# Four one-use landing places and groups of four in the expert stage of a two-layer decoder

## The reference

```python
def swiglu(x, w1, w3, w2):
    return (jax.nn.silu(x @ w1) * (x @ w3)) @ w2

logits = (t @ w_router).astype(jnp.float32)
top_v, top_i = lax.top_k(logits, TOP_K)          # 2 of 8
top_w = jax.nn.softmax(top_v, axis=-1)
combine = jnp.sum(jax.nn.one_hot(top_i, N_EXPERTS) * top_w[..., None], axis=1)
for e in range(N_EXPERTS):
    out = out + combine[:, e:e + 1] * swiglu(t, w1[e], w3[e], w2[e])
```

## Time and profile before

| | |
|---|---|
| median of 3 runs | 1219.22 us |
| profiled execution | 1219.02 us, span 1217.2 us |
| TensorE (PE) busy | 1202.1 us, 99% |
| VectorE (DVE) / ScalarE (ACT) busy | 737.4 us / 593.7 us |
| expert stage | from 550.65 us (first product) to about 1206.5 us |
| HBM read | 379.8 MB |

### The profile page before, as it was taken

How to read it: one execution, slowest core, us unless ns; L and a number is a source line. 1 busy time by engine, 2 the same in 40 slices (tenths; PEclk the granted TensorE clock), 3 DMA queues, 4 the chain that set the end, 5 groups by cost and what they waited for, 6 DMA issues and landing times.

```text
span 1217.2 us, 15724 instructions
## 1 busy us (share of the span) xinstructions
PE 1202.1 (99%) x6377; PEld 907.8 (75%) x6377; DVE 737.4 (61%) x769; ACT 593.7 (49%) x645; POOL 67.8 (6%) x55
## 2 busy tenths in 40 slices
PE   9999999999999999999999999999999999999996
PEld 8778888888888888888777666777567776667762
DVE  6867766656445857767665745755546664566532
ACT  6667435444436467446545434544535444454430
POOL 0600001000000600000000000000000000000001
PEclk9999999999999999999999999999999999999999
DMA  9753558555554454367999999999999999999997
GB/s 378 302 197 117 182 184 295 184 202 178 184 197 173 169 177 141 136 248 275 408 425 428 385 424 416 428 428 418 424 416 430 427 421 415 427 429 426 429 423 299
DMA packets 36590, 384.82 MB, mean 316 GB/s; under 512 B 4337, under 2 KB 4337, under 8 KB 7985
## 3 DMA queue, kind: packets, MB, share of 16 engines
q1 hardware_dynamic: 34672, 374.83, 76.8%
q0 software_dynamic: 1696, 8.66, 1.9%
q10 hardware_dynamic: 144, 0.26, 0.1%
HBM read 379.80 MB, written 7.61 MB: 318 GB/s over the span
## 4 chain that ended last, share of the span: by engine, by line
PE 91%; DMA 2%; DVE 2%; issue 2%; ACT 1%; POOL 1%; SPq 0%; DVEq 0%; ACTq 0%; POOLq 0%
PE ps L621 22%; PE ps L623 21%; PE ps L622 21%; PE ps L1728 18%; PE ps L1254 3%; DMA ring<-in_pairs 1%; PE ps L1624 1%; DMA h<-in_x 1%; PE ps L1612 1%; DVE wl L616 1%; POOL rst L759 1%; PE ps L1313 1%; ACT wh L598 0%; PE ps L1600 0%; DVE mix L2088 0%
## 5 line engine op out<-in xcount | busy, mean ns | idle before, releaser
L616 DVE TENSOR_TENSOR wl<-raw,wh 128x2048 fp32r<-128x2048 f32 x170 | 391.9, 2307 | 259.8 <-ACT wh L598 259.2
L598 ACT ACTIVATE wh<-raw 128x2048 fp32r<-128x2048 f32 x170 | 325.4, 1917 | 262.5 <-PE ps L623 243.6
L621 PE MATMUL ps<-wh,XT 128*128 128x512 f32 x856 | 341.7, 399 | 1.2 <-DVE wl L616 1.1
L623 PE MATMUL ps<-wh,XT 128*128 128x512 f32 x856 | 333.8, 390 | 0.0
L622 PE MATMUL ps<-wl,XT 128*128 128x512 f32 x856 | 333.6, 390 | 0.0
L621 PEld LDWEIGHTS ps<-wh,XT 128*128 128x128 f32 x856 | 160.7, 188 | 52.2 <-issue 16.2
L623 PEld LDWEIGHTS ps<-wh,XT 128*128 128x128 f32 x856 | 160.7, 188 | 34.5
L622 PEld LDWEIGHTS ps<-wl,XT 128*128 128x128 f32 x856 | 160.9, 188 | 30.9
L616 DVE TENSOR_TENSOR wl<-ring,wh 128x2048 fp32r<-128x2048 f32 x48 | 109.9, 2290 | 79.5 <-ACT wh L598 79.2
L598 ACT ACTIVATE wh<-ring 128x2048 fp32r<-128x2048 f32 x48 | 91.9, 1914 | 101.7 <-PE ps L623 90.8
L1728 PE MATMUL ps<-raw,few_X 128*64 128x256 f32 x768 | 88.2, 382 | 0.0
(11 more groups left out here) (296 smaller groups left out, 1151.9 us busy)
## 6 DMA issues: line engine op xcount, KB each, us to landing
raw<-in_pairs SPq DMA_DIRECT2D x76, 2048.0 KB, 13.1
ring<-in_pairs SPq DMA_DIRECT2D x52, 2048.0 KB, 13.5
raw<-in_units SPq DMA_DIRECT2D x86, 1024.0 KB, 4.9
raw<-in_lasts SPq DMA_DIRECT2D x6, 1024.0 KB, 13.6
y_rows<-in_zeros POOLq DMA_DIRECT2D x7, 512.0 KB, 7.9
raw<-in_boot SPq DMA_DIRECT2D x5, 512.0 KB, 7.1
y_rows<-xs POOLq DMA_DIRECT2D x4, 512.0 KB, 10.9
ring<-in_lasts SPq DMA_DIRECT2D x2, 1024.0 KB, 10.9
```

Of the source, the lines that this page charges most:

```text
L598: nc.scalar.activation(wh[:, U.split_slot(j), :], U.raw(j), ACT.Copy).then_inc(hi_ready, 1)
L616: nc.vector.tensor_tensor(wl[:, s, :], U.raw(j), wh[:, s, :].bitcast(F32), ALU.subtract).then_inc(lo_ready, 1)
L621: nc.tensor.matmul(o, xh, bh, start=start, stop=False)
L623: return nc.tensor.matmul(o, xl, bh, start=False, stop=stop)
```

## The change

Four units of expert 0 (s0.8, s0.9, s0.14, s0.15) are loaded singly into places of their own that are used once: behind the tables, in two parts of the mixer's memory, and in `xs`. Ten loads of expert 0 (16 units) now come before the first light pair; the ring's numbers count only the loads that go to the ring. Whole units are taken in groups of two pairs, as soon as four are due, and the load order is the taken order with one swap at each border, which moves the second light pair behind the split-form loads that follow it. By these functions there are 31 visits, the last of 15 units. `normed_rows` (four ScalarE copies into `hn`) moves ahead of `gathered_hi`, and the gather for the first light expert moves from the fifth unit of expert 0 to the third. The two parts of `moe_gT` are laid side by side in one tensor, and some small tables move to other addresses.

```diff
-FEW_FROM, FEW_ALONE = 6, 12
+FEW_FROM, FEW_ALONE = 4, 12
+FIRST_LOADS = [(0, 0, 2), (0, 2, 2), (0, 4, 2), (0, 6, 2), (0, 8, 1), (0, 9, 1), (0, 10, 2), (0, 12, 2), (0, 14, 1), (0, 15, 1)]
+ONCE = [(0, 8, 1), (0, 9, 1), (0, 14, 1), (0, 15, 1)]
@@ moe_orders
     for load in chain:
-        loaded.append(load)
-        taken.append(load)
         n += load[2]
         due = max(0, n - FEW_FROM) * (n_few - FEW_ALONE) // (n_chain - FEW_FROM)
-        while due - done >= few[0][2]:
-            loaded.append(few[0])
-            taken.insert(len(taken) - 1, few[0])
-            done += few.pop(0)[2]
-    return loaded + few, taken + few
+        while due - done >= few[0][2] + few[1][2]:
+            for _ in range(2):
+                taken.append(few[0])
+                done += few.pop(0)[2]
+        taken.append(load)
+    taken += few
+    loaded = [load for load in taken if load[0] != 0 or load[1] >= FIRST_LOADS[-1][1] + FIRST_LOADS[-1][2]]
+    for i in range(1, len(loaded)):
+        if loaded[i][0] in CHAIN and loaded[i - 1][0] in SMALL:
+            loaded[i - 1], loaded[i] = loaded[i], loaded[i - 1]
+    return FIRST_LOADS + loaded, taken
...
+RING_LOADS = [load for load in LOADS if load not in ONCE]
@@ places
+        once = [nc.alloc_sbuf_tensor_at(f"once_{k}", [P, UNIT], F32, offset=at)[:, :]
+                for k, at in enumerate((once_0_at, once_1_at, arena_at + 4 * ZV))] + [xs[:, :]]
@@ loads
+        def load_once(eng, p, j):
+            k = ONCE.index((p, j, 1))
+            if k == 0:
+                eng.wait_ge(ret_w, 4 * DEPTH)
+                eng.wait_ge(zr_ready, DEPTH)
+            elif k == 1:
+                eng.wait_ge(unit_used, MOE_BASE)
+            elif k == 2:
+                eng.wait_ge(logit, 2)
+            else:
+                eng.wait_ge(gat, 2)
+                eng.wait_ge(hn_rows, 2)
+            of = pairs_d[j // 2][:, j % 2 * UNIT:(j % 2 + 1) * UNIT]
+            eng.dma_start(once[k], of).then_inc(once_in[k], 16)
@@ load_ring
-            p, j, count = LOADS[i]
+            p, j, count = RING_LOADS[i]
             if i >= RING:
-                q, first, n = LOADS[i - RING]
+                q, first, n = RING_LOADS[i - RING]
@@ scalar
+            normed_rows()
             gathered_hi(0)
             for p, j in IN_USE:
-                if (p, j) == (0, 1):
-                    normed_rows()
```

More of the change, by code:

```diff
@@ L109 @@
 USED = {NUMBER[unit]: MOE_BASE + k + 1 for k, unit in enumerate(IN_USE)}
-LOAD_OF = {NUMBER[p, j + a]: (i, a) for i, (p, j, count) in enumerate(LOADS) for a in range(count)}
+RING_LOADS = [load for load in LOADS if load not in ONCE]
+LOAD_OF = {NUMBER[p, j + a]: ((p, j, count), a) for p, j, count in LOADS for a in range(count)}
 def is_whole(n):
@@ L151 @@
                          ("g_qk_t", 2 * DEPTH),
-                         ("freq", NF), ("mask", P), ("iota", P), ("before", P), ("fold", E), ("wr", KC * E),
+                         ("freq", NF), ("mask", P), ("iota", P), ("before", P), ("fold", E), ("wr", KC * E), ("pad", 2),
                          ("decay", HEADS * SEQ)])
@@ L221, in build @@
         place[0] = arena_at + 4 * (ZRV + 2 * UNIT)
-        gT_at = place[0]
-        moe_gT_h = over("moe_gT_h", FC * P, F32R)
-        moe_gT_l = over("moe_gT_l", FC * P, F32R)
         moe_sgm = over("moe_sgm", 512)
         moe_gbuf = over("moe_gbuf", 512)
+        gT_at = place[0]
+        moe_gT = over("moe_gT", FC * 2 * P, F32R)
+        once_1_at = place[0] - 4 * UNIT
+        assert once_1_at >= gT_at + 4 * 2 * P * 12 and once_1_at >= arena_at + 4 * (QKT + KC * SEQ)
         assert place[0] <= arena_at + 4 * MIX_WORDS
@@ L248, in build @@
         xs = sb("xs", [P, TT * D])
+        cols_at = (nc.sbuf_base + 31) // 32 * 32
         cols = sb("cols", [P, COLS_W])
+        once_0_at = cols_at + 4 * COLS_LAST
+        dead = sb("dead", [P, UNIT - (COLS_W - COLS_LAST)])
+        place[0] = cols_at + 4 * COLS_W
         ring_4_at = (nc.sbuf_base + 31) // 32 * 32
@@ L273, in build @@
         pos_f = sb("pos_f", [P, TT])
-        cos = sb("cos", [P, TT, NF])
-        sin = sb("sin", [P, TT, NF])
+        cos = over("cos", TT * NF)[:, :].rearrange("p (t f) -> p t f", t=TT)
+        sin = over("sin", TT * NF)[:, :].rearrange("p (t f) -> p t f", t=TT)
         ang = sb("ang", [P, 3, TT, NF])
@@ L278, in build @@
         pair = pair.rearrange("p (a r e) -> p a r e", a=3, r=MIDDLE)
-        turn_t = sb("turn_t", [P, DEPTH, 4, TT, 2, DA_HALF])
+        turn_t = over("turn_t", DEPTH * 4 * TT * 2 * DA_HALF)[:, :]\
+            .rearrange("p (l k t a d) -> p l k t a d", l=DEPTH, k=4, t=TT, a=2)
         g_subs = sb("g_subs", [P, DEPTH])
-        lamp = sb("lamp", [P, 2, DEPTH, HD])
+        lamp = over("lamp", 2 * DEPTH * HD)[:, :].rearrange("p (a l d) -> p a l d", a=2, l=DEPTH)
+        assert place[0] <= once_0_at + 4 * UNIT
         lams = sb("lams", [P, 2, DEPTH])
@@ L331, in build @@
         loaded = [sem(f"loaded{s}") for s in range(RING)]
+        once_in = [sem(f"once_in{k}") for k in range(len(ONCE))]
         hi_ready = sem("hi_ready")
@@ L530, in raw @@
                 if self.in_ring(j):
-                    i, half = LOAD_OF[n]
-                    return ring[i % RING][:, half * UNIT:(half + 1) * UNIT]
+                    of, half = LOAD_OF[n]
+                    if of in ONCE:
+                        return once[ONCE.index(of)]
+                    return ring[RING_LOADS.index(of) % RING][:, half * UNIT:(half + 1) * UNIT]
                 return raw[:, n % self.raw_slots, :]
@@ L538, in landed @@
                 if self.in_ring(j):
-                    i, _ = LOAD_OF[n]
+                    of, _ = LOAD_OF[n]
+                    if of in ONCE:
+                        return once_in[ONCE.index(of)], 16
+                    i = RING_LOADS.index(of)
                     return loaded[i % RING], 16 * (i // RING + 1)
@@ L675, in build @@
         gT3 = [g[:, :].rearrange("p (c t n) -> p c t n", c=FC, t=TT) for g in (gT_h, gT_l)]
-        moe_gT3 = [g[:, :].rearrange("p (c t n) -> p c t n", c=FC, t=1) for g in (moe_gT_h, moe_gT_l)]
+        moe_gT3 = [moe_gT[:, :].rearrange("p (c a t n) -> p a c t n", c=FC, a=2, t=1)[:, a] for a in range(2)]
         xs3 = xs[:, :].rearrange("p (t n) -> p t n", t=TT)
@@ L718, in _ @@
             e_of = {0: 0}
-            for i, (p, _, _) in enumerate(LOADS):
+            for p, j, count in LOADS:
+                if (p, j, count) in ONCE:
+                    load_once(sp, p, j)
+                    continue
                 if p not in e_of:
@@ L723, in _ @@
                     e_of[p] = sp.value_load(otab[0:1, 1 + BY_COUNT[p]:2 + BY_COUNT[p]], min_val=1, max_val=MIDDLE)
-                load_ring(sp, i, e_of[p])
+                load_ring(sp, RING_LOADS.index((p, j, count)), e_of[p])
             sp.wait_ge(table_ready, 1)
```

3 lines of the change are left out of this document (2 added, 1 removed).

## The result

The changed kernel takes **1283.64 us** (median of 4 runs, 1278.69 to 1287.78), the kernel before 1219.24 us beside it: a ratio of 1.053 (95% interval 1.0515 to 1.0545). It is slower by 64.4 us, where 20.3 us were forecast. The profiled execution took 1285.48 us with a span of 1283.8 us, 66.6 us more than the 1217.2 us before.

What follows compares the result with a forecast made beforehand. PE and the transfer line both looked full, PE a little faster. From 598.5 us, 605.9 - 4 + 24.7 = 626.6 us of transfers put the last landing at 1225; forecast 1219.2 + 20.3 = 1239.5 us, range 1218 to 1246.

Steps and rivals of the forecast that it cites:

- 24.7 us in which the line stands idle: Expert stage: sum of the transfer line's lapses at experts' ends and before the last 15 units, plus 0.9 us.
- the steady part: Between experts' ends: each visit's second half goes by the line, eight units in 19.6 us or more; no idle line.
- the places where an expert ends: Late-freed ring places idle the line: 6.8, 6.1 and 7.2 us at three ends, 3.7 before the last 15 units.
- What bounds the kernel: Expert stage: PE decides the middle, a little faster than the nearly full transfer line, and uses up its stock at the end.
- The four places: Start of the expert stage: a lead of some 14 us is lost at f2.6; worth 0 us, bounds +0.9 and -0.5.
- The visits: Expert stage: 60 visits become 31, taking 29 x 0.36 = 10.4 us of work from PE.
- normed_rows: Copies between two splits move ahead of the gather's end, removing PE's wait for a low part: gain 0.9 us.
- The second half of each visit waits: Mid-visit, PE waits for light units some 26 times, 0.6 to 3.9 us each, together about 32 us.
- The line: From the 24th unit at 598.5 us, transfers take 605.9 - 4 + 24.7 = 626.6 us; the last lands at 1225.
- The restart: A 2 MB load into an idle line lands after 7.7 us; with 7.5 us, some 3 us less in all.
- the visits' saving comes through: Rival, 12%: PE's 10 us of saved work make the kernel faster; 1208 us, or 1215 at best by the line.
- Slower by more: Rival, 4%: ScalarE and VectorE can't keep PE's pace, so split-form units wait as well; 10 us more, 1250.

Runs made afterwards that it cites:

- experiment 3: The kernel before with the four single-use places and the first ten loads, but its old taken order and load order: 1218.40 us, ratio 0.9996.
- Experiment 8: The changed kernel with its load order kept, but each load goes into the place that comes free first: 1231.91 us, ratio 1.0096.
- Experiment 5: The changed kernel with the second light load behind one split-form load at each border, not two: 1223.91 us, ratio 1.0042.
- Experiment 7: Both kernels, transferring only half of each pair from the ring's eleventh load on: changed kernel 1212.64 us, kernel before 1216.62 us.
- experiment 9: The changed kernel with visits beginning two split-form units earlier, loads sorted by when they are wanted, places as they come free: 1213.20 us, ratio 0.9951.
- experiment 1: The changed kernel with loads in the taken order, without the swap at each border: 1272.64 us, ratio 1.0443.

## Why the prediction was wrong in size

The direction and the mechanism were right, the size was not: +64.4 us against +20.3, outside the range of 1218 to 1246. The step that failed is the term "24.7 us in which the line stands idle". In its place the line lost 83.8 us (18.9 before). The term was counted along a beat of PE that no wait disturbs. That left out two things: in **the steady part** ("The loads are issued early enough to keep the line itself busy") it had nothing, and at **the places where an expert ends** it had each lapse once, without what PE's waits do to the places given up next. A price that is missing altogether is the clock's.

*What bounds the kernel.* Right. With half the bytes the kernel before takes 1216.62 us, 2.2 less than the one beside it: PE alone sets all but 2.2 us of the time. That the line has hardly more to spare is read from its share of 0.99 to 1.01.

*The four places: 0.* Right, 0.9996 in experiment 3. The reasons were right as well: f2.6 issued at 591.3 (forecast 590.8), landed at 598.9 (598.5), as its turn and not its room decides. In the changed order they do save 6 us, which the prediction did not see.

*The visits: -10.4, and normed_rows: -0.9.* Too large; together 4.0. The price of 0.36 us came from visits with no transposes in them. In groups of four, the transposes fall into the middle of many visits, 0.35 us dearer each, and 2.7 us of load waits stay even with half the bytes. 11.3 - 4 - 2.7 = 4.6 us, against the 4.0 measured.

*The second half of each visit waits.* Right in place and number: 25 waits for loads, each in a visit, about 26 forecast. Their sum is 51.2 us, not about 32.

*The line.* It loses 64.9 us more than before, where 20.7 were forecast (24.7 less today's 4). I had followed the ring once through an undisturbed beat of PE. But a wait of PE moves the release of the next place, the load for that place goes out later by as much, and with places in turn everything behind it does too; the chain from 677 to 714 us above shows one full turn of this. The first round of it can be read off, though the first lapse is no wait's doing: f2.8 went out 5.95 us behind f2.6, by the ring's order alone, and landed 6.70 us behind it, 1.8 us lost. The prediction had s0.18's place given up 14.5 us into the visit, in the third visit at 614.2 + 14.5 = 628.7 us; f2.14, for that place, was issued at 633.53 us, since the visit had lasted 12.13 us and not 7.4. The load before it had landed at 635.2 us, f2.14 at 641.3. By 661.9 us it had landed 48 units, where I counted 50 by 663. The visit placed at 676.5 us began at 680.3; the issue of s1.2, placed at 691.2, came at 699.50, and the idle stretch of the line that I had near 681 to 683 us came at 697 to 700. In the steady stretches, where I had put nothing, 11.5 us went (3.2 + 2.7 + 5.6), and at the three ends and the last units 53.4 us, for 19.8 (6.8, 6.1, 7.2 and 3.7, less the 4 of today). So three quarters of what the term lacked were at the ends. Of the idle time, how much is this circle and how much are lapses that a full count without it would have found was not separated.

Today's own loss was misread too: by the table it is 18.9 us, where the sum took off 4. With 18.9 taken off, the same count would have come to about 1225 us. That error brought the forecast nearer to the result, by luck.

Experiment 8 shows that the fixed turn of the places is a part of the cause, and not the order alone: the same loads in the same order lose 13 us instead of 64 when a load may take the place that comes free first. Experiment 5 shows the other part: with the light load behind one split-form load instead of two, PE waits for loads 2.7 us in all, and 5 us of the 64 are left.

*The restart.* The prediction took 7.7 us for a 2 MB load into an idle line. Five loads of 2 MB that went out into an empty line took 7.58 (f2.6), 7.68 (s1.8 and s3.2), 7.66 (s5.2) and 7.72 us (f7.22), so that term stands as a rule. But s1.2, issued at 699.50 into an empty line, took 9.00 us. The 7.8 us of the earlier trace rows is not quite such a case, as the load before it landed only at 680.5. The Trainium skill, "DMA: Bandwidth & Descriptors", section on the anatomy of one DMA, would have given 6.8 us with its fit for the GpSimd path; no load here is that fast.

*Missing altogether: the clock.* Twelve waits, of 1.28 to 4.54 us, ended in 3.4 us at half the clock, which costs PE 1.7 us each. Held up, it gives 10.4 us back. The Trainium skill, "TensorE: Matmul & The Clock Gate", section on oscillation, tells of a kernel in which every wait for the next tile brings the clock down again, at the cost of half the time spent low. The trace agrees on the price (5.36 for 3.67 us), but not every wait had it here: five waits of 1.5 to 2.5 us passed at the full clock. By that price, 12 x 1.7 = 20.4 us were PE's, of which half shows in the time. The other half, I suppose, would have been spent waiting for the line; that was not tested by itself.

*The sum by PE*, within the profiled executions: load waits 51.2 - 1.3, the low part -0.9, the clock +20.4, and the span's +66.6 leaves -2.8 us for the visits. Experiment 7 has more for them: 4.0 + 2.7 - 0.9 = 5.8 us. So 3 us of this sum are not accounted for.

*Rivals.* That the visits' saving comes through (12%) was wrong as the kernel stood, but of the two conditions named for it, experiment 9 met one: its line is ahead at the start, by 12.5 us at the 24th unit, and the time is 5.7 us less than that of the kernel before beside it. Its lapses are not gone: by the count of landings it loses 25.4 us from the 24th unit on, more than the 18.9 of before. "Slower by more" (4%) had the sign, but late splits as its cause; in the changed kernel PE waited for no low part. They do appear when the loads stand in order of use (experiment 1), as late small steps of VectorE behind splits whose load is late.

*Left open.* Why the order of loads costs 13.6 us even with free places: the profile has 18.6 us of load waits there, but from a slower execution than the median. A part of that execution is the clock's: between 889 and 902 us PE worked 12.51 of 13 us at a granted clock of 0.50. And the order that `ring_places` writes comes from a count with two fixed prices; how near it is to the best was not tried.

## What to carry to other kernels

When both PE and the transfer line are full, follow the ring of buffers for two rounds and not one, the second with the delays of the first: a wait moves the release of a buffer, and with places in fixed turn every load behind the one that needs it. Look at which load stands at the head of an in-order queue, and for whose buffer; with buffers in fixed turn a small misorder (one load of 2 MB in each visit, one step too late) cost 60 us here, and a free choice of buffer took 52 us off without touching the order. Add the clock to the price of each wait of TensorE, and price a step inside a group by rows of that form.

## What the runs showed of the hardware

Of the 17 waits of PE of 1.28 us or more after 600 us, 12 ended in a granted clock of 0.50 for 3.4 us; the shortest of them was 1.28 us, and one of 2.48 us passed without. None of the shorter ones (up to 1.02 us) did it. The stretches were not 3.4 us long everywhere: in experiment 8 one lasted 13.7 us, from the end of a wait of 3.1 us on. 226 matmuls of 128 columns, spread over the waits, brought the mean from 0.983 to 0.998. And the changed kernel's time was less steady than that of before: 1278.7 to 1287.8 us over 4 runs (0.7%), against 0.1 to 0.3% over the 13 to 19 runs of the kernel before beside the experiments. Why was not tested.
